# Moving the token-factor product behind a quarter of the third weight piece, and giving the token shifts precedence in a hand-written order of work

## The reference, cut to what matters

```
h = rmsnorm(x, norm_mix_g)              # x * rsqrt(mean(x*x) + eps) * g
u = h @ w_in                            # 1024 x 5376
u_rwkv, u_attn, u_gate = split(u)       # 1792, 1536, 2048 columns
# rwkv7_time_mix starts with a token shift:
prev = u_rwkv moved down by one token
c = u_rwkv + (prev - u_rwkv) * mu
r, k, v, wd, ad, gd = split(c)          # 512, 512, 512, 64, 64, 128
w = -softplus(-(w0 + tanh(wd) @ w2)) - 0.5 ;  a = sigmoid(a0 + ad @ a2) ; g = sigmoid(gd) @ g2
# then a recurrence over the tokens (done in chunks of 64 with small products), group norm and gate
# u_attn feeds a causal differential attention, u_gate two sigmoid gates;
# all meet in  x + (g_a*(o_a @ w_proj_a) + g_b*(o_b @ w_proj_b)) @ w_out
```

## Time and profile before

| | |
|---|---|
| median of 3 runs | 1415.07 us (1415.0 to 1415.1) |
| the profiled execution's own time | 1414.93 us |
| its span | 1413.1 us |
| PE busy, DVE busy, ACT busy | 1403.6, 1178.3, 816.8 us |
| TensorE's granted clock, mean of the span | 0.999 of full speed |

### The profile page before, as it was taken

How to read it: one execution, slowest core, us unless ns; L and a number is a source line. 1 busy time by engine, 2 the same in 40 slices (tenths; PEclk the granted TensorE clock), 3 DMA queues, 4 the chain that set the end, 5 groups by cost and what they waited for, 6 DMA issues and landing times.

```text
span 1413.1 us, 22864 instructions
## 1 busy us (share of the span) xinstructions
PE 1403.6 (99%) x9163; PEld 1194.0 (84%) x9163; DVE 1178.3 (83%) x1645; ACT 816.8 (58%) x1109; POOL 28.2 (2%) x93
## 2 busy tenths in 40 slices
PE   8999999999999999999999999999999999999999
PEld 7988778888888888889878888888888887888887
DVE  6876686898877898998868888988889798688897
ACT  6735474565446555555766565555555557665562
POOL 1000000000001100000000000000000000000000
PEclk9999999999999999999999999999999999999999
DMA  9441235456555555455434555545555444355543
GB/s 345 175 150 63 91 120 208 176 183 205 193 220 179 186 202 186 172 208 194 139 118 176 182 194 188 211 167 200 200 179 196 166 177 147 112 202 193 182 176 119
DMA packets 37257, 250.16 MB, mean 177 GB/s; under 512 B 4256, under 2 KB 4384, under 8 KB 8096
## 3 DMA queue, kind: packets, MB, share of 16 engines
q1 hardware_dynamic: 36864, 248.51, 49.2%
q10 hardware_dynamic: 288, 0.19, 0.1%
HBM read 247.64 MB, written 1.05 MB: 176 GB/s over the span
## 4 chain that ended last, share of the span: by engine, by line
PE 97%; DVE 1%; DMA 1%; ACT 0%; SPq 0%; issue 0%; POOL 0%; DVEq 0%; ACTq 0%; POOLq 0%
PE ps L2253 24%; PE ps L2172 16%; PE ps L2174 15%; PE ps L2173 15%; PE ps L2260 13%; PE ps L2425 2%; PE ps L2237 1%; PE ps L2241 1%; PE ps L2243 1%; PE ps L2337 1%; PE ps L2638 1%; PE ps L2618 1%; PE ps L2627 1%; DMA raw<-ws 1%; PE ps L2410 0%; PE ps L2562 0%
## 5 line engine op out<-in xcount | busy, mean ns | idle before, releaser
L3058 DVE TENSOR_TENSOR lo<-raw,hi 128x2048 fp32r<-128x2048 f32 (+1 forms) x230 | 522.1, 2270 | 61.1 <-ACT hi L2681 58.3
L2681 ACT CAST hi<-raw 128x2048 fp32r<-128x2048 f32 (+1 forms) x230 | 436.6, 1899 | 190.0 <-PE ps L2174 119.8
L2253 PE MATMUL ps<-h,hi 128*128 128x512 f32 x1504 | 359.0, 390 | 0.0
L2253 PEld LDWEIGHTS ps<-h,hi 128*128 128x128 f32 x1504 | 276.4, 188 | 52.5
L2172 PE MATMUL ps<-hi,a 128*128 128x512 f32 x516 | 205.1, 397 | 0.0
L2174 PE MATMUL ps<-hi,a 128*128 128x512 f32 x516 | 201.4, 390 | 0.0
L2173 PE MATMUL ps<-lo,a 128*128 128x512 f32 x516 | 201.2, 390 | 0.0
L2260 PEld LDWEIGHTS ps<-h,lo 128*128 128x128 f32 x1504 | 192.2, 190 | 7.9
L2260 PE MATMUL ps<-h,lo 128*128 128x256 f32 x1504 | 194.4, 282 | 0.0
L2885 ACT COPY a<-ps 128x256 f32<-128x256 f32 x208 | 75.9, 372 | 144.4 <-PE ps L2253 78.8
L2172 PEld LDWEIGHTS ps<-hi,a 128*128 128x128 f32 x516 | 96.9, 188 | 22.6 <-issue 2.4
(11 more groups left out here) (379 smaller groups left out, 1852.9 us busy)
## 6 DMA issues: line engine op xcount, KB each, us to landing
raw<-ws SPq DMA_DIRECT2D x227, 1024.0 KB, 4.8
raw<-ws SPq DMA_DIRECT2D x4, 512.0 KB, 8.3
X<-xin SPq DMA_DIRECT2D x8, 256.0 KB, 7.1
raw<-ws SPq DMA_DIRECT2D x4, 256.0 KB, 5.8
out<-X SPq DMA_DIRECT2D x4, 256.0 KB, 2.1
small<-small SPq DMA_DIRECT2D x1, 992.5 KB, 7.4
const<-const SPq DMA_DIRECT2D x1, 900.0 KB, 8.0
a<-xtin SPq DMA_DIRECT2D x3, 256.0 KB, 5.8
```

The costliest lines, as they stand in the source:

```text
L2253: t = e.matmul(b2(s["slots"][u]), wh[:, k, 128 * u:128 * u + 128], h2[:, k, :, :], start=k == 0, stop=last)
L2681: e.copy(hi[j % NSPL][:, n], raw[j % NRAW][:, n]).then_inc(hi_ready, 1)
L3058: e.tensor_tensor(lo[j % NSPL][:, n], raw[j % NRAW][:, n], hi[j % NSPL][:, n].bitcast(F), ALU.subtract).then_inc(lo_ready, 1)
```

## The change

Three edits. In `first_piece`, the step given as `between` (for the third piece: the product of the tokens' factors and its copy to RB) is now emitted after the first group of that piece's products and no longer before it; the piece takes its PSUM bank first. The planner's time is set to DVE's clock ahead of that step. And the track `shifts` gets the lead of 10.0 that the recurrence's tracks have.

```diff
             yield from room(1)
-            if between:
-                between()
             sl = take()
             for n, (which, k0, k1, waits) in enumerate(FIRST[i]):
                 emit("first", ...)
+                if between and n == 0:
+                    between()
                 if n < len(FIRST[i]) - 1:
                     yield "pe"
...
                     def known():
+                        cur[0] = max(cur[0], due["dve"])
                         nm.rows()
                         to_shift.extend(early)
                         early.clear()
...
-        weave([shifts(), rwkv_decays(), rwkv_keys(), (rwkv_chain(), LEAD), (rwkv_block(0), LEAD), ...
+        weave([(shifts(), LEAD), rwkv_decays(), rwkv_keys(), (rwkv_chain(), LEAD), (rwkv_block(0), LEAD), ...
```

## The result

The changed kernel takes 1421.25 us in the median of 5 runs (1420.15 to 1423.02); before, 1415.08. The ratio is 1.0045 (95% interval 1.0034 to 1.0055): it is slower by 6.2 us, where 1.3 us of gain were forecast. The profiled execution took 1421.25 us with a span of 1419.4. Since the diff adds a line, a line of the changed kernel has a number one higher than before: `lora` is L2367, `shift` L3200, the cast of a piece L2682, its low part L3059.

What follows compares the result with a forecast made beforehand. PE, busy 99%, was taken as the bound. Removing its first wait and shortening the second by a third put PE 1.30 us ahead at `lora`, further reordering at nothing: 1413.8 us, 8 in 10 within 1412.2 to 1415.4.

Steps and rivals of the forecast that it cites:

- (a): DVE's list at the start: the low part stays ahead of `shift`, `lora` 0.9 us later, 1416.0 us; chance 0.08.
- a reshuffle that I don't see: Unspecified reordering, one of two ways to be slower by over 0.2%; the chance for both together was 0.06.
- the last of its signs of being wrong: A gap at the mixer's end that differs from the one at `lora` by more than 1.2 us.
- `lora` 0.14 later: 28.75: First `lora` on PE: starts 0.14 us after `lora_in` ends at 28.61, so at 28.75 instead of 30.05.
- What the order does further on: From `lora` to the mixer's end: 35 runs of small products rewoven, 1.2 us either way, taken as nothing.
- (b): Mixer's end: recurrence's `oa_lo` over 2.94 us later makes `w_proj_a` wait; 5 us later gives 1415.9 us; chance 0.12.
- (d): Nothing is left: the early gain goes at another wait or on more small-product runs, 1415.0 us; chance 0.08.
- the sentence on strict first-in, first-out queues: DVE's list near 23 us: piece 3's low part can't pass the waiting copy to RB, which comes 0.90 us later.

Runs made afterwards that it cites:

- no. 1: Changed kernel without the lead of the shifts, the other two edits kept: 1415.38 us, ratio 1.0005.
- no. 8: Changed kernel without the shifts' lead, and with the first `lora` waiting for the small weights only, not the constants: 1415.05 us, ratio 0.9999.
- no. 10: Changed kernel without the shifts' lead, and with `lora`'s own 256 KB of small weights sent first on their own semaphore: 1414.37 us, ratio 0.9994.
- no. 3: Changed kernel with weight piece 16's DMA held until the third product step behind piece 13's low part: 1418.09 us, ratio 1.0023.
- no. 9: Changed kernel with the fourth head's `d_lo` right behind its high part, ahead of the second eviction and piece 22's low part: 1420.07 us, ratio 1.0038.
- no. 11: Changed kernel with piece 16's DMA held, `d_lo` right behind its high part, and `lora`'s 256 KB of weights sent first: 1414.77 us, ratio 0.9999.
- no. 2: Kernel before with the lead of the shifts alone: 1428.6 us, ratio 1.0092.
- no. 6: Changed kernel with piece 22's low part moved behind the fourth head's `d_lo` in DVE's list: 1421.07 us, ratio 1.0045.
- no. 5: Kernel before with weight piece 17's DMA issued some 1.8 us later, over an instruction fetch: 1415.12 us, ratio 0.9998.
- no. 4: Changed kernel with the first `lora` waiting for the small weights alone, no longer for the constants: 1419.81 us, ratio 1.0033.
- no. 12: Changed kernel without setting the planner's time to DVE's clock ahead of the factors' product: 1425.23 us, ratio 1.0072.
- no. 7: Changed kernel with first `lora` waiting for small weights only, piece 16's DMA held, and piece 22's low part behind `d_lo`: 1416.68 us, ratio 1.001.

## Why the prediction was wrong

**Right:** edit 1 and edit 2 on PE, DVE and ACT. The product needs no wait, `shift` follows the copy, the low part follows it, and each start is within 0.2 us. Rival (a) did not come. The outcome lies where the prediction had put 0.06, "a reshuffle that I don't see", and the last of its signs of being wrong is met: the mixer's end is 6.27 us later and `lora` 0.14 earlier.

**The first step that failed** is "`lora` 0.14 later: 28.75". It took `lora` to wait for `lora_in` alone, as the waits of before had it. But such a row names only what came last. The DMA view of before holds the other condition; its columns are KB and the median us from issue to landing:

```profile
21.96 0.43 SPq L3703 DMA_DIRECT2D const<-const  x1
...
const<-const SPq DMA_DIRECT2D x1, 388.0 KB, 7.9
```

21.96 + 7.9 = 29.86, against `lora_in`'s end at 29.91: two conditions 0.05 us apart, and only one was moved. Nos. 1, 8 and 10 show it, each taking off one layer: `lora` starts at 29.91 with the constants, at 29.06 with the small weights alone, and at 28.52, by `lora_in`, when its own 256 KB come first. Of 1.30 us forecast, 0.14 were left; the step was 1.16 us too early.

**The second, and the dearer,** is "What the order does further on", which counted 35 runs of small products and put the new weave at nothing, with 1.2 us either way. The count was about right (36 runs after), and it was the wrong measure. A new order changes not only how often forms alternate but what meets what: which DMA is in flight when instructions are fetched, and what stands ahead of a low part that PE wants. Two such meetings, with the half clock behind one, made up to 2.41 + 1.71 + 1.64 = 5.76 us. Nos. 3, 9 and 11 show that; no. 1 shows that they come only with the lead, and no. 2 that the lead without edits 1 and 2 brings others.

**Rivals (b) and (d)** were near in kind and wrong in place. (b) had a chain end too late at the mixer's end, but that of the recurrence at `w_proj_a`: `oa_lo` came at 205.23, earlier than at 206.84. The late one was the attention's, which the prediction left out although the same weave orders it: its last `d_lo` came 15.8 us later. (d) was argued away by "behind `lora` the trace has no wait in which a gain could vanish". That is so of the old order, and says nothing of the new one.

Of the sentence on strict first-in, first-out queues in the prediction (the Trainium skill, "TensorE: Matmul & The Clock Gate", "Architectural detail: the array is 16x 32x32, not 1x 128x128"): it was applied to the copy at 23 us, and it is what decides at 203 us too. In no. 6 `d_lo`, whose high part was done at 199.83, before DVE's idle 1.97 us began, stands behind an eviction that waits for PE, and PE then waits for `d_lo`. The trace agrees.

On the fetch, the Trainium skill ("Runtime: NRT & Kernel Launch", "Instruction fetch mechanics") says that each engine's sequencer fetches its program in 16 KiB blocks over a DMA queue of its own while it executes, and that the cost is mostly hidden. The packets of 16 KB on queue q8 agree, and so do before and no. 5, which show no stop; the 2.2 to 2.4 us stops of the changed kernel and of nos. 4, 6, 9 and 12 don't: there the cover ended, with a weight DMA's packets in front of the fetch. Weights in front are not enough (no. 5), and no. 7 shows a stop of 0.31 us without them.

Left open: the 0.65 us of the account, which is no accident of one profile: less the stop and the wait for `d_lo` where they occur, nos. 3, 9 and 11 too take 0.7 to 0.9 us more than before from `lora` to the mixer's end, and nos. 1 and 10, without the lead, 0.4 and 0.7. Open is also why the clock falls behind the stop in some executions and not in others, and how late a fetch may be at other places than the one at 95 us; 0.76 us (no. 5) did no harm.

## What to carry to other kernels

Before a wait is costed as gained, read every condition of the waiting instruction and the time at which each is met: the view of waits names only the last one, and a transfer that lands 0.05 us ahead of it takes the gain. A change of precedence in a planned order is not a local edit; its price can't be counted from the old trace, so treat it as of unknown sign and several microseconds wide, or change the order by hand at the one place that is wanted. And where a low part stands behind an eviction that waits for PE, PE ends up waiting for itself, whatever is taken off the engine between.

## What the runs showed of the hardware

A single fetch of 16 KB of instructions can stop PE for 2.3 us. In six profiles (after, nos. 4, 6, 7, 9 and 12) PE goes on 2.2 to 2.6 us behind the fetch's start, though the packet itself takes about 1 us: 95.08 to 97.39, 95.18 to 97.56, 95.07 to 97.29, 92.05 to 94.68, 95.14 to 97.35, 98.83 to 101.20. In all six the run of 64 breaks off after 59 products, so it seems to be one place of the program. The profile puts such a stop down to "issue", and only the DMA queue `instruction` shows its cause.

An idle stretch of 2.3 us was followed by 3.4 us at half clock in two profiles (after, and no. 12) and not in three others with the same stop (nos. 4, 6 and 9). The half clock in the first 15 us doesn't tell them apart: it lasted 6.8 us in those three and 3.4 in after, but in no. 12 PE's products too follow each other at 0.21 us, the pace of the half clock, from 7.0 to 12.8 us. Three longer gaps between PE's starts were all followed by half clock: 4.4 and 4.6 us in no. 2 (3.4 and 6.8 us), 4.2 us at `lora` in no. 12 (3.4 us); one of 2.9 us at `lora` in no. 3 was not. The 5 runs of the changed kernel differ by 2.9 us between each other, the 5 of before by 0.3. The coming and going of this stretch, worth up to 1.7 us, may be a part of it, but nos. 1 and 3, whose profiles have no stop, scatter by 2.5 and 2.4 us as well; the cause of the scatter stays open.
